# RWKV group norm, bonus and gate moved into the chunk stage; output-projection rows loaded ahead and split row by row

## What is computed

```python
    y = rwkv7_recurrence(rh, split_heads(decay, RWKV_HEADS), kh, vh, kk, split_heads(a, RWKV_HEADS))
    mean = jnp.mean(y, -1, keepdims=True)
    var = jnp.mean(jnp.square(y - mean), -1, keepdims=True)
    y = ((y - mean) * lax.rsqrt(var + RWKV_GN_EPS)).reshape(b, s, RWKV_WIDTH)
    y = y * ln_w + ln_b
    bonus = jnp.sum(rh * kh * r_k.astype(jnp.float32), -1, keepdims=True) * vh
    return ((y + bonus.reshape(b, s, RWKV_WIDTH)) * g).astype(p.dtype)
...
# both layers:  x = x + mixer_output @ w_out ; then the router and the experts
```

## Time and profile before

| | us |
|---|---|
| median of 3 executions | 2985.09 |
| lowest, highest | 2984.51, 2987.57 |
| the profiled execution, whole | 2982.0 |
| its span in the trace | 2980.3 |
| last RWKV turn and tail, before the finish phase | 567 to 601 |
| `rwkv_finish`, first DMA issue to last DVE instruction | 603.1 to 668.7 |
| start of layer 0's `moe` to its first projection matmul | 670.3 to 698.3 |
| start of layer 1's `moe` to its first projection matmul | 2140.2 to 2168.2 |

### The profile page before, as it was taken

How to read it: one execution, slowest core, us unless ns; L and a number is a source line. 1 busy time by engine, 2 the same in 40 slices (tenths; PEclk the granted TensorE clock), 3 DMA queues, 4 the chain that set the end, 5 groups by cost and what they waited for, 6 DMA issues and landing times. The chain is left out here.

```text
span 2980.3 us, 53818 instructions
## 1 busy us (share of the span) xinstructions
PE 2598.4 (87%) x18812; PEld 2161.0 (73%) x18812; DVE 1937.3 (65%) x2177; ACT 1583.0 (53%) x1832; POOL 394.0 (13%) x342
## 2 busy tenths in 40 slices
PE   5997899956979999999468999999489899999990
PEld 4775799925858888888357888888376688888880
DVE  3358255543379999899535666566435799989984
ACT  3656123222148888788323555554312588788871
POOL 0020000000002333332010000000000133333320
PEclk9999899977989999999779999999599899999995
DMA  3110000004259999999510111110222799999974
GB/s 97 45 36 29 22 4 4 4 4 165 86 182 371 381 385 384 384 376 356 201 50 26 32 29 36 29 29 15 103 76 85 275 379 378 383 381 385 383 275 182
DMA packets 219978, 525.16 MB, mean 176 GB/s; under 512 B 43825, under 2 KB 99121, under 8 KB 219825
## 3 DMA queue, kind: packets, MB, share of 16 engines
q1 hardware_dynamic: 201392, 489.34, 44.1%
q0 software_dynamic: 18432, 33.60, 3.0%
HBM read 506.06 MB, written 50.33 MB: 187 GB/s over the span
## 5 line engine op out<-in xcount | busy, mean ns | idle before, releaser
L1640 DVE TENSOR_TENSOR w_low<-w_raw,w_high 128x1024 fp32r<-128x1024 f32 x768 | 894.9, 1220 | 28.0 <-DVEq L52 18.3
L1358 ACT CAST w_high<-w_raw 128x1024 fp32r<-128x1024 f32 x768 | 755.2, 1050 | 104.4 <-ACTq L52 104.0
L1506 PE MATMUL ps<-w_high,x_high 128*128 128x512 f32 x1024 | 413.5, 404 | 7.3 <-PEq L52 6.5
L1510 PE MATMUL ps<-w_high,x_low 128*128 128x512 f32 x1024 | 402.5, 393 | 0.0
L1509 PE MATMUL ps<-w_low,x_high 128*128 128x512 f32 x1024 | 400.5, 391 | 0.0
L1506 PEld LDWEIGHTS ps<-w_high,x_high 128*128 128x128 f32 x1024 | 194.7, 190 | 49.9 <-issue 13.7
L1901 PE MATMUL ps<-h_high,w_high 128*128 128x512 f32 x512 | 212.5, 415 | 16.2 <-PEq L52 16.2
L1510 PEld LDWEIGHTS ps<-w_high,x_low 128*128 128x128 f32 x1024 | 193.4, 189 | 42.8
L1509 PEld LDWEIGHTS ps<-w_low,x_high 128*128 128x128 f32 x1024 | 194.3, 190 | 37.2
L1506 PE MATMUL ps<-w_high,hidden_high 128*128 128x512 f32 x512 | 200.9, 392 | 6.7 <-PEq L52 6.7
L1901 PE MATMUL ps<-h_high,w_low 128*128 128x512 f32 x512 | 202.1, 395 | 0.0
(11 more groups left out here) (399 smaller groups left out, 5057.4 us busy)
## 6 DMA issues: line engine op xcount, KB each, us to landing
w_raw<-in_moe_w_gate SPq DMA_DIRECT2D x256, 512.0 KB, 5.2
w_raw<-in_moe_w_up SPq DMA_DIRECT2D x256, 512.0 KB, 5.7
w_raw<-in_moe_w_down SPq DMA_DIRECT2D x256, 512.0 KB
w_raw<-expert_rows SPq DMA_DIRECT2D x32, 512.0 KB, 10.1
w_tiles<-in_c_w_in SPq DMA_DIRECT2D x32, 512.0 KB, 4.0
w_tiles<-in_ab_w_in SPq DMA_DIRECT2D x22, 512.0 KB, 4.0
residual<-in_x SPq DMA_DIRECT2D x16, 512.0 KB, 8.8
h_rows<-hn_moe SPq DMA_DIRECT2D x16, 512.0 KB, 2.9
```

Source lines behind the costliest of these rows:

```text
L1358: act.copy(wh[:, p, :], raw[:, p, :]).then_inc(high_made, 1)
L1506: ins = pe.matmul(ps[:, bank, :], high, w_h, start=first, stop=False)
L1510: return pe.matmul(ps[:, bank, :], low, w_h, start=False, stop=final)
L1640: dve.tensor_tensor(wl[:, p, :], raw[:, p, :], wh[:, p, :].bitcast(F32), ALU.subtract).then_inc(low_made, 1)
```

## The change

1. `rwkv_finish` is gone. Its work is cut into eight units of one 128-channel block by 512 tokens (`units`, first half of the tokens first) inside `rwkv_chunks`. The products r\*k\*r_k (`product`) run on DVE in turns 1 to 4, the eight bonus sums (`head_sum`) on PE and the eight products with v (`bonus_rows`) on DVE in the last turn. The rest runs in and behind the tail: PE multiplies y by a centring matrix (`centre`: identity minus head mean, so no separate mean), ACT squares it out of PSUM (`square`), PE sums the squares (`variance`), ACT makes the reciprocal root with Ln and Exp (`inverse_root`), DVE does three instructions (`finish`), PE makes the gate (`gates`). In the tail, `u` of the last chunk now stands ahead of `y_rows` of the one before.
2. `g2` is loaded at the start of the phase. When the last turn's inversion is done, SP loads layer 0's eight output-weight rows into `w_out_rows`, a place that so far held the inversion's tiles, and that the next phase does not overwrite.
3. In `moe`, both layers: `y_part(0)` and `y_rest(0)` come ahead of the eight casts and subtractions, `y_part(1)` and `y_rest(1)` behind them. `project` now takes its passes in the order high x high, low y x high weight, high y x low weight, and its first call waits for each `wo_high` and `wo_low` row as it comes to it. `par_in` is waited for only ahead of the first `logits`. In layer 0 the weight rows come from `w_out_rows`, and only the residual rows are loaded at the start of the phase.

```diff
-def rwkv_chunks(nc, c, proj, b):
+def rwkv_chunks(nc, c, a, proj, b):
...
+            @block.sync
+            def _(sp):
+                sp.dma_start(g2[:], a["rw_g2"][0]).then_inc(g2_in, 16)
+                sp.wait_ge(x_next, 2 * NLV * NTURN)
+                sp.wait_ge(mk_done, NTURN)
+                for q in range(KT):
+                    sp.dma_start(c.w_out_rows[:, q, :], a["ab_w_out"][0][q * P:(q + 1) * P, :]).then_inc(c.w_out_in[q], 16)
...
+                def centre(u):
+                    h, j = units[u]
+                    pe.wait_ge(y_copied, 2 * NTURN // NH * (h + 1))
...
+                    if u >= 2:
+                        pe.wait_ge(scaled, u - 1)
+                    pe.matmul(ps[:, B_C[u % 2], :], centring[:], y[:, j, half(u)], start=True, stop=True).then_inc(centred, 1)
...
                 f = NTURN - 1
-                for ci in range(2):
-                    u(f, ci)
-                    sa(f, ci)
-                    if ci == 0:
-                        ds(f, ci)
-                    y_rows(f, ci)
+                u(f, 0)
+                centre(0)
+                sa(f, 0)
+                centre(1)
+                ds(f, 0)
+                variance(0)
+                gates(0)
+                u(f, 1)
+                y_rows(f, 0)
+                variance(1)
+                centre(2)
+                sa(f, 1)
+                gates(1)
+                centre(3)
+                y_rows(f, 1)
...
+                def square(u):
+                    act.wait_ge(centred, u + 1)
+                    if u >= 2:
+                        act.wait_ge(var_summed, u - 1)
+                    act.activation(sq[:, u % 2, :], ps[:, B_C[u % 2], :], ACT.Square).then_inc(squared, 1)
+
+                def inverse_root(u):
+                    act.wait_ge(var_summed, u + 1)
+                    if u >= 2:
+                        act.wait_ge(scaled, u - 1)
+                    act.activation(rs[:, u % 2, :], ps[:, B_V[u % 2], :], ACT.Ln, bias=eps[:, 0:1], scale=1.0 / HD).then_inc(log_done, 1)
+                    act.wait_ge(log_done, u + 1)
+                    act.activation(rs[:, u % 2, :], rs[:, u % 2, :], ACT.Exp, scale=-0.5).then_inc(rstd_done, 1)
...
+                def finish(u):
...
+                    dve.wait_ge(rstd_done, u + 1)
...
+                    dve.scalar_tensor_tensor(out=o, in0=ps[:, B_C[u % 2], :], scalar=b.ln_w[:, j:j + 1], in1=rs[:, u % 2, :],
+                                             op0=ALU.mult, op1=ALU.mult).then_inc(scaled, 1)
+                    dve.wait_ge(scaled, u + 1)
+                    ch(dve.scalar_tensor_tensor(out=o, in0=o, scalar=b.ln_b[:, j:j + 1], in1=bonus[:, j, half(u)],
+                                                op0=ALU.add, op1=ALU.add))
+                    dve.wait_ge(g_summed, u + 1)
+                    dve.tensor_tensor(o, o, ps[:, B_GATE[u % 2], :], ALU.mult).then_inc(gated, 1)
...
                 for k in range(KT):
-                    sp.dma_start(raw[:, k, :], w_out[k * P:(k + 1) * P, :]).then_inc(raw_in[k], 16)
+                    if not early:
+                        sp.dma_start(raw[:, k, :], w_out[k * P:(k + 1) * P, :]).then_inc(raw_in[k], 16)
...
+                y_part(0)
                 for k in range(KT):
-                    take(act, raw_in[k], 16)
-                    act.copy(wo_h[:, k, :], raw[:, k, :]).then_inc(wo_high, 1)
-                    if k < 2:
-                        y_part(k)
+                    if early:
+                        act.wait_ge(c.w_out_in[k], 16)
+                    else:
+                        take(act, raw_in[k], 16)
+                    act.copy(wo_h[:, k, :], w_rows[:, k, :]).then_inc(wo_high, 1)
+                y_part(1)
...
-                    for ys, wp in ((xh, wo_h), (xh, wo_l), (xl, wo_h)):
+                    for ys, wp, ready in ((xh, wo_h, wo_high), (xl, wo_h, None), (xh, wo_l, wo_low)):
                         for k in range(KT):
+                            if t == 0 and h == 0 and ready is not None:
+                                pe.wait_ge(ready, k + 1)
...
-                pe.wait_ge(par_in, 64)
-                pe.wait_ge(wo_low, KT)
```

More of the change, by code:

```diff
@@ L829, in _ @@
                         rows(f + 1, 0)
+                    else:
+                        head_sum(0)
                     dx(f, 0)
@@ L833, in _ @@
                         rows(f + 1, 2)
+                    else:
+                        head_sum(1)
+                        head_sum(2)
                     t1(f, 1)
@@ L839, in _ @@
                         gram_b(f + 1, 0)
+                    else:
+                        head_sum(3)
                     t1(f, 2)
@@ L845, in _ @@
                         gram_b(f + 1, 1)
+                    else:
+                        head_sum(4)
+                        head_sum(5)
                     t1(f, 3)
@@ L856, in _ @@
                         gram_k(f + 1)
+                    else:
+                        head_sum(6)
+                        head_sum(7)
                     dx(f, 4)
@@ L1005, in _ @@
                     level(f, 4)
+                    if f == 0:
+                        dve.scalar_tensor_tensor(out=centring[:], in0=c.head_ones[:], scalar=-1.0 / HD, in1=c.ident[:], op0=ALU.mult,
+                                                 op1=ALU.add).then_inc(consts, 1)
+                        dve.memset(eps[:], GN_EPS).then_inc(consts, 1)
+                    if not nxt:
+                        for u in range(3):
+                            bonus_rows(u)
                     if seq:
@@ L1009, in _ @@
                     masks_r(f)
+                    if 1 <= f < 5:
+                        product(f - 1)
+                    if not nxt:
+                        bonus_rows(3)
+                        bonus_rows(4)
                     x_add(f, 3)
@@ L1012, in _ @@
                         x_start(f + 1)
+                    else:
+                        bonus_rows(5)
                     x_add(f, 4)
@@ L1102, in moe @@
-def moe(nc, c, a, layer, y, w_out, next_gain, fetch=None, h_high=None, h_low=None, out=None):
+                for u in range(len(units)):
+                    finish(u)
+def moe(nc, c, a, layer, y, w_out, next_gain, fetch=None, early=False, h_high=None, h_low=None, out=None):
     gain = a["norm_ffn"][layer]
```

197 lines of the change are left out of this document (113 added, 84 removed).

## The result

The changed kernel takes **2942.9 us** (median of 4 executions, 2941.9 to 2945.0), against 2985.9 (4, 2984.5 to 2987.6) for the kernel before: ratio 0.9852, 95% interval 0.9839 to 0.9865. The profiled execution took 2943.2, its span 2941.4.

The account below looks back on a forecast made before the run. No engine was taken as the limit; the engines wait for each other. Terms of -15.2 (chunk stage), -21.8 (layer 0) and -6.4 us (layer 1) sum to -43.4, from 2985.1 to 2941.7 us, range 2932 to 2954.

Parts of the forecast that it names:

- the term of the chunk stage: From the last turn to the `moe` start: starts at 655.1 instead of 670.26, -15.2 us (-9.5 to -19).
- Last turn: Chunk stage's last turn: added `head_sum` and `bonus_rows` lengthen it by 7.5 us (5.5 to 9).
- The products of turns 1 to 4: The four `product` on DVE, behind the masks where DVE sits idle: cost nothing; 1.2 us if the cover fails.
- Tail and finish: Behind the last turn: one chain carried by ACT, 54.3 us from the tail's first `u`, ending at 652.5 (649 to 658).
- Its sign, ACT without idle time: Sign of being right: sixteen 1.28 us table loads between about 605 and 650, ACT the engine without idle time there.
- Boundary: Between the chunk phase and layer 0's `moe`: one barrier instead of two, with 37 semaphore clears, about 2.6 us.
- Layer 0's start: Layer 0's `moe`: first projected half 14.2 us behind the phase's start against 36.0, -21.8 us (-20 to -24).
- Layer 1: Layer 1's `moe`: first pass done behind the casts, 16 cold matmuls remain, -6.4 us (-3 to -9).
- Cold or long chain: Rival, chance 0.17: tail at 1.2 GHz (+4.5), last turn +1.5, layer 0 +1.2, layer 1 +3.4; about 2952 us.
- no table-load cost: Rival, chance 0.03: Ln and Exp share a table, walk ends 20.5 us earlier less 4 us of waits; 2925 us.
- Late small tensors: Rival, chance 0.07: gain rows or `par_in` arrive late, and PE waits at `project(1, 0)`; 2948 us.
- slower: Rival, chance 0.02: row-paced first pass keeps TensorE at 1.2 GHz through the projection behind it; 3006 us with one layer.

Follow-up runs that it names:

- the first trace: The changed kernel's first profiled execution, unedited: 2943.2 us.
- the second trace: The changed kernel run once more for a trace, nothing edited: 2943.8 us once.

## Why the prediction was right, and where not

The forecast was 2941.7 (2932 to 2954), the median is 2942.9. Its three terms predicted -43.4 us, and they measured -36.4 (+10.5 and -19.0, -20.5, -7.4 in the table); two things outside them made up the difference. In the traces another 2.5 us were won elsewhere (+2.0, -8.4 and +3.9), and the profiled execution of before lay 3.9 us below its median while that of after lay 0.3 above. So that the whole came within 1.2 us of the forecast is luck. The terms of the two projections' starts were right; the term of the chunk stage was wrong: -15.2 forecast with a range of -9.5 to -19, -8.5 measured. Two of its steps failed.

- **Last turn, +7.5 forecast (5.5 to 9), +10.5 measured, of which in the first trace 1.4 lie in turns 4 to 6.** The matmuls' price was right: 8 x 0.86 = 6.9 against 6.7. The step that failed took `bonus_rows` as a delay of DVE only. The three-bank reuse of `B_SUM` makes PE wait for it, 2.1 us, and in the second trace the clock that fell behind it is worth another 1.5. "What is put into it adds to it" held for waits too.
- **The products of turns 1 to 4, nothing: right**, as the kernel without sums shows.
- **Tail and finish.** From the first copy to the end 52.9 us were forecast and 56.3 measured. The step that failed is the sum of ACT's waits in the ring, with its allowance for the clock. Roots: 3.94 against 3.9. To the first table load 7.3 against 6.0 from the copy. Waits of ACT: 1.32, 2.53, 3.01 and 3.02 us ahead of squares 3, 5, 6, 7 and 1.1 ahead of the last y copy, 11.0 us, where 6.8 and a 2.5 allowance for the clock stood. The allowance was taken from a mean clock of 0.77; the mean was 0.83, but the clock was near 0.50 just where `centre` lay on the path. The end came at 660.8 instead of 652.5 (649 to 658); the remaining 4.9 us had come from ahead. The claim that ACT carries the chain was half right: ACT holds 3.94 + 0.6 of a period of 7.55, and the chain goes round through DVE and PE. Its sign, ACT without idle time, did not show.
- **Boundary:** 660.82 to 663.70, 2.9 against 2.6.
- **Layer 0's start, -21.8 forecast, -20.5 measured.** The first half came at s+15.5. That is the end of the range for PE at 1.2 GHz, 15.4: the whole second pass (3.62) and part of the third (2.72) were at the low clock. Taking the middle was the error; a pass paced by casts, with 0.15 us of idle time ahead of each matmul, did not bring the clock up. The gain rows landed at s+14.6, where s+13 to s+16 stood: no time lost, and 0.8 us to spare. Two of the signs of being wrong, a row that names the gain rows ahead of the first add and a clock of 0.5 in the projection, showed, the second in the first half only.
- **Layer 1, -6.4 forecast, -7.4 measured.** The second pass was at the low clock, the third (2.18) nearly at the high one, where the forecast had both at the low one; that is the 1 us. In the ten traces with this start the gain is 5.0 to 7.7 us.
- **The rivals.** "Cold or long chain", 2952, came in good part: 3.4 of its 4.5 us in the tail, its last turn, its cold layer 0, but not its layer 1. The total doesn't show it, since other things covered it. The condition of "no table-load cost", 2925, did not come: the trace has all sixteen loads. The nearest experiment, one activation instead of two, took out fifteen loads and eight activations: 2920.4, a gain of 21.6 to 22.5 where the walk had 20.5 less 4 for the loads alone. A period fell by 3.94: 3.25 are the root, 0.95 the clock, which the shorter ring kept at 1.00, less 0.26 of a new wait. "Late small tensors" didn't come. In the "slower" one the clock would have stayed low beyond the first half; it rose inside it, in both layers.
- **A cited row.** The cold price was put at twice 0.86 on the strength of 6 records in 4.43 us, which is 1.48 for a matmul. Twice 0.86 was right nevertheless: two such matmuls start 1.71 us apart in the changed kernel (649.80, 651.51).

The Trainium skill, "ScalarE: Activation LUTs", section "What ACT_TABLE_LOAD costs", asks for 1.38 us of drain at every switch. The trace disagrees, as it had before the change: Ln's 0.69 us from 644.41, the load at 645.11, Exp at 646.40, so a whole switch takes 1.30 us. The kernel with one activation a root has fifteen such switches fewer, 19.5 us, and eight activations fewer, 5.0 us, and it won 22.5, not twice that.

Outside the terms, part of the gain goes along with the granted clock. In eleven windows of 50 us of layer 1's mixer the clock is below full for 13.5 and 14 us in the two traces of before (50 us times the missing share, summed) and for 10 us in the changed kernel's, whose stretch is 5.0 to 5.5 us shorter. Two experiments with 13 and 14 us lie between, at 547.7 and 548.5. Why a kernel changed elsewhere meets it differently, and where the +2.9 us in layer 1's experts comes from, isn't settled; the clock is seen to go along with the time, not shown to cause the difference.

## What to carry to other kernels

When work on several engines is cut into units and pipelined, write down the ring: who frees the buffer that the next unit needs, and through which engines that release runs. If it passes through all of them, the period is the sum of their times, every shortened step shortens it by its whole length, and the cheapest gains are a step taken out (here two table loads and an activation, 3.25 us per unit) and one buffer more (2.7 us of the finish here). Ask of each link whether it is data or only the order of a list: here two of them were order, and no run tried another. Before splitting a large phase, count the operations whose price doesn't shrink with the unit: two table loads became sixteen.

When a small job is put into a turn that PE bounds, price its waits as well as its matmuls: moving three VectorE instructions ahead of one level was worth more than half of the sums' own cost.

## What the runs showed of the hardware

- A reciprocal on VectorE of 128x512 fp32 took 3.35 us, where a multiply of the same size took 0.75. Taking reciprocal and root in one ScalarE activation took 0.69.
- TensorE's granted clock may or may not be 0.50 behind the same idle time of 2.14 us in the same place (1.71 against 1.15 us for the 32 matmuls behind it): it fell in six traces of eight, and the changed kernel's two traces are one of each kind.
- Eight 512 KB transfers did not lengthen the part of the tail in which they ran: 12.81 us with and without.
